# A modulation product whose weight blocks are half split for TensorE, and loaded first

## What is computed

```
shift, scale, gate = silu(c) @ w_ada + b_ada        # w_ada is 1024 x 3072; two conditioning vectors
h = rmsnorm(x) * (1 + scale) + shift
p = h @ w_in                                         # queries, keys, values and gates of two branches
... two attention branches, merge, output projection, residual, final norm
```

## Time and profile before

| | us |
|---|---|
| runs, median (lowest to highest of 3) | 1250.15 (1248.86 to 1251.68) |
| the profiled execution, its own time | 1253.08 |
| its span in the profile | 1251.2 |
| TensorE busy in the span | 1217.1 |
| VectorE busy | 833.5 |
| ScalarE busy | 603.2 |
| mean granted TensorE clock | 0.994 of full |

### The profile page before, as it was taken

One profiled execution on the slowest core, in us unless ns is written; L12 is line 12 of the kernel. 1 busy time (PEld: TensorE's weight loads), 2 busy tenths in 40 slices (PEclk: granted clock), 3 DMA queues, 4 the chain that ended last, 5 costly groups with the idle time before them and its releaser, 6 DMA issues.

```text
span 1251.2 us, 21399 instructions
## 1 busy us (share of the span) xinstructions
PE 1217.1 (97%) x7488; PEld 1087.1 (87%) x7488; DVE 833.5 (67%) x1644; ACT 603.2 (48%) x1207; POOL 189.9 (15%) x203
## 2 busy tenths in 40 slices
PE   7999999999999999999999999999999999999997
PEld 1499889988998999899889989989988898998996
DVE  2368468765875776687687688678768876454452
ACT  3342235544553545265455456546547574443341
POOL 0000023120402130231000000000000025433430
PEclk9999999999999999999999999999999999999999
DMA  9345633132204213221611111321013277543530
GB/s 360 146 175 167 230 109 97 54 132 94 98 34 149 94 69 109 90 96 52 190 62 39 53 39 55 99 69 53 26 51 110 62 242 252 170 147 121 195 141 34
DMA packets 81100, 142.90 MB, mean 114 GB/s; under 512 B 7047, under 2 KB 58119, under 8 KB 81037
## 3 DMA queue, kind: packets, MB, share of 16 engines
q1 hardware_dynamic: 66636, 119.92, 28.7%
q10 hardware_dynamic: 14400, 22.15, 4.9%
HBM read 106.65 MB, written 35.40 MB: 114 GB/s over the span
## 4 chain that ended last, share of the span: by engine, by line
PE 76%; DVE 12%; ACT 4%; issue 4%; DMA 2%; SPq 0%; ACTq 0%; DVEq 0%; POOL 0%
PE d_ps_pairs L86 20%; PE s_ps_pairs L86 11%; PE y_ps L1783 9%; PE b_ps L86 9%; PE o_ps_pairs L1016 7%; PE t_ps_pairs L985 6%; PE v_ps L86 6%; PE s_ps_pairs L944 3%; PE s_ps_pairs L943 3%; DMA wada<-in_w_ada 2%; DVE pt L1335 2%; PE v_ps L299 2%; DVE mn L1345 1%; DVE s_ps_pairs L1352 1%; ACT pr L1141 1%
## 5 line engine op out<-in xcount | busy, mean ns | idle before, releaser
L86 PE MATMUL d_ps_pairs<-h,wt 128*128 128x384 f32 (+2 forms) x1920 | 352.1, 338 | 0.9 <-ACT craw L1159 0.9
L86 PEld LDWEIGHTS d_ps_pairs<-h,wt 128*128 128x128 f32 x1920 | 316.7, 188 | 16.0 <-ACT craw L1159 1.4
L1335 DVE TENSOR_TENSOR pt<-t_ps_pairs,pt 128x512 fp32r<-128x512 f32 (+1 forms) x272 | 157.6, 621 | 39.1 <-ACT pt L1117 37.8
L86 PE MATMUL s_ps_pairs<-h,wt 128*128 128x512 f32 (+1 forms) x864 | 168.4, 354 | 0.0
L1141 ACT ACTIVATE pr<-s_ps_pairs,mx 128x896 f32<-128x896 f32 x128 | 128.2, 1004 | 69.7 <-DVE mx L1361 40.1
L86 PEld LDWEIGHTS s_ps_pairs<-h,wt 128*128 128x128 f32 x864 | 141.6, 189 | 21.7
L1117 ACT ACTIVATE pt<-t_ps_pairs 128x512 fp32r<-128x512 f32 (+1 forms) x272 | 134.1, 548 | 14.8 <-PE t_ps_pairs L985 9.9
L985 PE MATMUL t_ps_pairs<-ident_sb,pr 128*128 128x128 f32 x960 | 131.5, 275 | 3.6 <-DVE pt L1335 2.4
L985 PEld LDWEIGHTS t_ps_pairs<-ident_sb,pr 128*128 128x128 f32 x960 | 107.8, 140 | 14.9 <-DVE pt L1335 10.5
L1783 PE MATMUL y_ps<-wo,mg 128*128 128x512 f32 x480 | 113.2, 396 | 0.0
L1783 PEld LDWEIGHTS y_ps<-wo,mg 128*128 128x128 f32 x480 | 90.0, 188 | 21.6
(11 more groups left out here) (174 smaller groups left out, 1710.3 us busy)
## 6 DMA issues: line engine op xcount, KB each, us to landing
wraw<-in_w_gate SPq DMA_DIRECT2D x24, 512.0 KB, 3.5
gt<-gates_d SPq DMA_DIRECT2D x40, 256.0 KB, 4.3
comb_a<-in_bias SPq DMA_DIRECT2D x24, 384.0 KB, 3.9
gates_d<-craw ACTq DMA_DIRECT2D x48, 192.0 KB, 1.9
vw_a<-v_d SPq DMA_DIRECT2D x64, 128.0 KB
v_d<-vst SPq DMA_DIRECT2D x20, 320.0 KB, 4.6
wada<-in_w_ada SPq DMA_DIRECT2D x12, 512.0 KB, 5.6
oz<-gates_d SPq DMA_DIRECT2D x20, 256.0 KB, 4.4
```

Source lines behind the costliest of these rows:

```text
L86: mm = eng.matmul(out, lhs(a, k), rhs(b, k), start=(k == 0 and i == 0), stop=(k == n_k - 1 and i == 2))
L1335: dve.tensor_tensor(pt[:, 1, c * 512:c * 512 + cols], t_ps[:, n % 2, 0:cols], pt[:, 0, c * 512:c * 512 + cols].bitcast(F32), ALU.subtract) ...
```

## The change

Blocks with an even k in either half (8 of the 16) are no longer multiplied in fp32. ScalarE writes their high part (`mod_high`) and VectorE their low part (`mod_low`), into space of `hm` that is unused at that time. The silu columns are split as well, into a stationary `scl` of 128 by 4 (two high columns, two low columns). A split block is four fp32r products of 512 columns: two chunks, each with the high and the low part of the weight. They write four rows of PSUM; the blocks with an odd k stay in fp32 and add to the first two rows. So four rows are copied to `modrow`, and `columns` turns each 128 of them into two columns by two ordinary fp32 products with parts of the identity, which also add the low rows to the high ones; before it was one transpose.

The loads are put in another order: all 16 modulation blocks, then the key weight, all six value pieces, then the second tokens. The slots are released accordingly: a split block's slot by its low part, an fp32 block's by its products. TensorE now does the columns of the shift half ahead of (1,6), takes (1,5) ahead of (1,4), and does the two first token transposes around the columns of the scale half. ScalarE makes both copies of the shift rows, in place of VectorE; its first squares alternate with `mod_high`. The splits of the first value pieces move: piece 0's and 1's low parts stand between the scale half of `modf` and the first `parts` on VectorE, and piece 2's stands behind the eighth `parts`.

```diff
-    modrow = h32[0:2, :, :]
+    scl = left["scl"]
+    modrow = h32[0:4, :, :]
...
-    SHIFT, KEYS, VALUES0, SCALE, VALUES1 = 0, 8, 9, 12, 20
+    SHIFT, SCALE, KEYS, VALUES = 0, 8, 16, 17
+    MODS = [(0, k) for k in range(KD)] + [(1, k) for k in (0, 1, 2, 3, 5, 4, 6, 7)]
+    SPLIT = [(half, k) for half in range(2) for k in (0, 2, 4, 6)]
...
+    def released(eng, n):
+
+        half, k = n // KD, n % KD
+        if (half, k) in SPLIT:
+            eng.wait_ge(mod_lo, SPLIT.index((half, k)) + 1)
+        elif k == KD - 1:
+            eng.wait_ge(mod_mm, 2 * half + 2)
+        else:
+            eng.wait_ge(ada_used, MODS.index((half, k)) - half + 1)
+
+    def mod_part(j, part):
+
+        return hm[:, part, j, 0:D]
...
         for k in range(4, KD):
             load_ada(0, k)
-        load_keys()
-        for m in range(3):
-            load_v(m)
         for k in range(KD):
             load_ada(1, k)
+        load_keys()
+        for m in range(6):
+            load_v(m)
         load_x(1)
-        for m in range(3, 6):
-            load_v(m)
         sp.wait_ge(wv_lo, 6)
         load_x(2)
...
         def modulation(half, k):
 
-            ring_wait(pe, (SHIFT, SCALE)[half] + k)
+            n = (SHIFT, SCALE)[half] + k
+            if (half, k) in SPLIT:
+                j = SPLIT.index((half, k))
+                pe.wait_ge(mod_lo, j + 1)
+                for c in range(2):
+                    for part in range(2):
+                        mm = pe.matmul(v_ps[0:4, 2 * half + c, :], scl[:, k, :], mod_part(j, part)[:, c * 512:(c + 1) * 512],
+                                       start=(k == 0 and part == 0), stop=False, skip_group_check=True)
+                mm.then_inc(ada_used, 1)
+                return
+            ring_wait(pe, n)
             for c in range(2):
-                mm = pe.matmul(v_ps[0:2, 2 * half + c, :], scol[:, k, :],
-                               ring((SHIFT, SCALE)[half] + k)[:, c * 512:(c + 1) * 512],
-                               start=(k == 0), stop=(k == KD - 1))
-            mm.then_inc(ada_used, 1)
+                mm = pe.matmul(v_ps[0:2, 2 * half + c, :], scol[:, k, :], ring(n)[:, c * 512:(c + 1) * 512],
+                               start=False, stop=(k == KD - 1), skip_group_check=True)
+                if k == KD - 1:
+                    mm.then_inc(mod_mm, 1)
+            if k < KD - 1:
+                mm.then_inc(ada_used, 1)
...
-                mm = pe.transpose(mod_ps[:, 2 * blk:2 * blk + 2], modrow[:, b // 4, (b % 4) * P:(b % 4 + 1) * P],
-                                  ident[0:2, 0:2])
+                for part in range(2):
+                    mm = pe.matmul(mod_ps[:, 2 * blk:2 * blk + 2], modrow[:, b // 4, (b % 4) * P:(b % 4 + 1) * P],
+                                   ident[0:4, 2 * part:2 * part + 2], start=(part == 0), stop=(part == 1))
...
-        pe.wait_ge(silu_done, 1)
-        for k in range(KD):
-            modulation(0, k)
-        pe.wait_ge(ident_in, 16)
-        for k in range(4):
-            modulation(1, k)
-        columns(0)
-        for k in range(4, KD - 1):
-            modulation(1, k)
+        pe.wait_ge(scl_done, 2)
+        for half, k in MODS:
+            if (half, k) == (1, 6):
+                pe.wait_ge(ident_in, 16)
+                columns(0)
+            modulation(half, k)
         transposed(0)
+        columns(1)
         transposed(1)
-        modulation(1, KD - 1)
-        columns(1)
         pe.wait_ge(wk_lo, 1)
...
+        def mod_high(j):
+
+            half, k = SPLIT[j]
+            ring_wait(act, (SHIFT, SCALE)[half] + k)
+            act.activation(mod_part(j, 0), ring((SHIFT, SCALE)[half] + k), ACT.Copy).then_inc(mod_hi, 1)
+
         act.wait_ge(small_in, 32)
         act.activation(scol[:, :, :], ccol[:, :, :], ACT.Silu).then_inc(silu_done, 1)
         act.wait_ge(const_set, 1)
+        mod_high(0)
+        mod_high(1)
         for t in range(XG[0][1]):
             square(0, t)
+            if t < 3:
+                mod_high(t + 2)
+        mod_high(5)
         root(0)
+        mod_high(6)
+        act.wait_ge(mod_mm, 2)
+        for c in range(2):
+            act.activation(modrow[:, c, :], v_ps[0:4, c, :], ACT.Copy).then_inc(mod_row, 1)
+        mod_high(7)
         ring_wait(act, KEYS)
         act.activation(wkb[:, 0, :], ring(KEYS), ACT.Copy).then_inc(wk_hi, 1)
-        for m in range(3):
-            values_high(m)
-        act.wait_ge(ada_used, 2 * KD)
+        values_high(0)
+        act.wait_ge(mod_mm, 3)
         act.wait_ge(mod_col, 1)
-        act.activation(modrow[:, 0, :], v_ps[0:2, 2, :], ACT.Copy).then_inc(mod_row, 1)
+        act.activation(modrow[:, 0, :], v_ps[0:4, 2, :], ACT.Copy).then_inc(mod_row, 1)
+        values_high(1)
         act.wait_ge(mod_ready, 2)
         for i in range(KD):
             modulate(i)
+            if i == 1:
+                values_high(2)
...
+                if g == 0 and t == 2:
+                    mod_low(6)
                 dve.tensor_scalar(x(g)[:, t, :], x(g)[:, t, :], rstd[:, t0 + t:t0 + t + 1], None, ALU.mult
                                   ).then_inc(xn_done, 1)
+
+        def mod_low(j):
+
+            half, k = SPLIT[j]
+            dve.wait_ge(mod_hi, j + 1)
+            dve.tensor_tensor(mod_part(j, 1), ring((SHIFT, SCALE)[half] + k), mod_part(j, 0).bitcast(F32), ALU.subtract
+                              ).then_inc(mod_lo, 1)
 
...
+        dve.wait_ge(silu_done, 1)
+        dve.tensor_copy(scl[:, :, 0:2], scol[:, :, :]).then_inc(scl_done, 1)
+        dve.wait_ge(scl_done, 1)
+        dve.tensor_tensor(scl[:, :, 2:4], scol[:, :, :], scl[:, :, 0:2].bitcast(F32), ALU.subtract).then_inc(scl_done, 1)
+        for j in range(6):
+            mod_low(j)
         normalise(0)
-        dve.wait_ge(small_in, 32)
-        dve.wait_ge(ada_used, KD)
-        for c in range(2):
-            dve.tensor_copy(modrow[:, c, :], v_ps[0:2, c, :]).then_inc(mod_row, 1)
+        mod_low(7)
         dve.wait_ge(wk_hi, 1)
         dve.tensor_tensor(wkb[:, 1, :], ring(KEYS), wkb[:, 0, :].bitcast(F32), ALU.subtract).then_inc(wk_lo, 1)
-        for m in range(3):
-            values_low(m)
+        dve.wait_ge(small_in, 32)
         dve.wait_ge(mod_col, 1)
         dve.tensor_tensor(modf[:, 0:KD, :], mods[:, 0:KD, :], bias[:, 0:KD, :].to_broadcast([P, KD, 2]), ALU.add
                           ).then_inc(mod_ready, 1)
-        dve.wait_ge(ada_used, 2 * KD)
+        dve.wait_ge(mod_mm, 4)
         dve.wait_ge(mod_row, 3)
-        dve.tensor_copy(modrow[:, 1, :], v_ps[0:2, 3, :]).then_inc(mod_row, 1)
+        dve.tensor_copy(modrow[:, 1, :], v_ps[0:4, 3, :]).then_inc(mod_row, 1)
         dve.wait_ge(mod_col, 2)
         dve.scalar_tensor_tensor(out=modf[:, KD:, :], in0=mods[:, KD:, :], scalar=1.0,
                                  in1=bias[:, KD:, :].to_broadcast([P, KD, 2]), op0=ALU.add, op1=ALU.add
                                  ).then_inc(mod_ready, 1)
+        values_low(0)
+        values_low(1)
         for i in range(KD):
             parts(i)
+        values_low(2)
         normalise(1)
...
+            small["scl"] = sb(first, "scl", [P, KD, 4], F32R, "right")
```

More of the change, by code:

```diff
@@ L125, in front @@
     ring_in = [sem(f"ring_in{i}") for i in range(RING)]
-    silu_done, ada_used, mod_row, mod_col, mod_ready = (
-        sem(n) for n in ("silu_done", "ada_used", "mod_row", "mod_col", "mod_ready"))
+    silu_done, scl_done, mod_hi, mod_lo, ada_used, mod_mm, mod_row, mod_col, mod_ready = (
+        sem(n) for n in ("silu_done", "scl_done", "mod_hi", "mod_lo", "ada_used", "mod_mm", "mod_row", "mod_col", "mod_ready"))
     sq_done, rms_done, rstd_done, xn_done, xt_done = (
@@ L150, in ring_wait @@
         eng.wait_ge(ring_in[n % RING], 16 * (n // RING + 1))
+    def released(eng, n):
[8 more added lines that the diff above has]
+        return hm[:, part, j, 0:D]
     def values_raw(n):
         k0, nk = VK[n % 3]
-        return ring(VALUES0 + n if n < 3 else VALUES1 + n - 3)[:, 0:nk * HW].rearrange("p (k c) -> p k c", c=HW)
+        return ring(VALUES + n)[:, 0:nk * HW].rearrange("p (k c) -> p k c", c=HW)
     def values_split(n, part):
@@ L180, in load_ada @@
             n = (SHIFT, SCALE)[half] + k
[L181 to L186, removed]
+            if n >= RING:
+                released(sp, n - RING)
             sp.dma_start(ring(n), io["w_ada"][k * P:(k + 1) * P, half * D:(half + 1) * D]).then_inc(ring_in[n % RING], 16)
         def load_keys():
-            sp.wait_ge(ada_used, KEYS - RING + 1)
+            released(sp, KEYS - RING)
             sp.dma_start(ring(KEYS), io["w_kb"]).then_inc(ring_in[KEYS % RING], 16)
         def load_v(m):
-            n = VALUES0 + m if m < 3 else VALUES1 + m - 3
-            used = n - RING if n < SCALE else KD + n - RING - SCALE
-            sp.wait_ge(ada_used, used + 1)
+            n = VALUES + m
+            released(sp, n - RING)
             k0, nk = VK[m % 3]
@@ L423, in values_high @@
         def values_high(m):
```

(2 more changed lines are left out.)

## The result

| | us |
|---|---|
| before, median of 7 (lowest to highest) | 1250.15 (1248.86 to 1252.51) |
| after, median of 7 (lowest to highest) | 1255.65 (1253.84 to 1257.22) |
| ratio, 95% interval | 1.0043 (1.0031 to 1.0055) |
| profiled execution after: own time, span | 1256.8, 1254.9 |

The kernel became slower by 5.5 us, where I had forecast 1.9 less. The range, 1244.8 to 1252.5, didn't hold it.

What follows compares the result with a forecast made beforehand. TensorE, busy 97% of the span, was taken as the bound. Gain 2.4 up to `modf`, less 1.3 for value splits, plus 0.85 in the loop: 1.95, so 1251.1 us profiled, 1248.2 as median (2.9 lower); range 1244.8 to 1252.5.

Steps and rivals of the forecast that it cites:

- Loads: First stage: in the new load order (1,0) lands at 21.1 instead of 26.0, so the 3.08 us stall goes.
- Splits: Modulation products: a split block costs 0.93 us against 1.72, so eight save 6.3 us of TensorE.
- rival E: Split blocks: a four-column fp32r pass costs an fp32 pass, so six splits save nothing; 1252.9 us, chance 0.03.
- The clock in the stall: Behind the first tokens: TensorE's stall brings one low-clock stretch of 3.4 us, doing 1.7 us less work.
- rival A: Stall at 16 us: TensorE idles under 2 us and the clock survives; gain 3.65, 1246.5 us, chance 0.20.
- The columns' own price: Columns of each half: 32 passes take 3.9 us, standing 0.12 apart.
- Rival B: Columns: passes run at the transposes' pace, 1.6 us less in each half; gain 5.15, 1245.0 us, chance 0.20.
- rival C: Columns: an ordinary fp32 product takes four times a transpose, 4.6 us a half; gain 0.55, 1249.6 us, chance 0.08.
- The value splits: Between `modf` and the first `parts` on VectorE: low parts of pieces 0 and 1 come first, loss 1.3 us.
- The loop: Loop over eight chunks: half of the 1.7 us lost to the low clock comes back, gain 0.85.
- The signs of being wrong: Columns at 0.07 or at least 0.14; from 12 to 40, clock 1.00 or 0.50 for over 6 us; repeated low-part waits.
- Rival D: Clock low from about 18 until 25 behind the stall, and 6.7 us in the loop; 1252.4 us, chance 0.12.

Runs made afterwards that it cites:

- the late columns: The kernel after, with the shift half's columns taken behind (1,7) instead of ahead of (1,6); 1258.04 us, ratio 1.007; its profiled execution took 1253.71.
- the first experiments: Early follow-up measurements, beside which 24 runs of the unchanged kernel before were taken; those runs' mean granted clock was 0.995 to 0.998.

## Why the prediction was wrong, step by step

**Loads: right.** The wait for (1,0) is gone, and no block was late: TensorE's chain from 18.5 to 44 has no DMA in it. The load order alone gave 4.4 us.

**Splits: right in kind, a tenth of a us short per block.** The stall ended at 18.54 (18.3 forecast), ScalarE and VectorE were never late behind it. A split block at full clock took 1.02 to 1.09 (0.93), an fp32 block 1.81 in this stretch (1.72), so rival E is out, and TensorE came to the columns at 34.3 and not at 33.3.

**The clock in the stall: right.** The mean of the first window row is 3.4 low us in five, as assumed; one block took 3.21 instead of 1.81. Six of seven profiled executions with this stall had it; in the seventh (the late columns) it did not come, as rival A had it, though not for A's reason: TensorE idled 2.3 us there too.

**The columns' own price: nearly right.** 32 passes at full clock took 3.67 (the run with the late columns) against my 3.9. Rival B, the transposes' pace (2.3), is out. So is rival C (4.6) at full clock: the traces give a factor of 3, about 0.22 for the two passes of an ordinary product and 0.071 for a transpose. That the kernel after took 4.44 is no point for C, as the clock was halved in the last 1.7 us of it. The rule of the Trainium skill behind it ("TensorE: Matmul & The Clock Gate", Terms) gives a factor of 4. My reason for 0.12, that the weight load sets the pace, isn't shown: a load shows as 187 ns there, and the passes stand 0.112 apart.

**The step that failed** is in the sum behind the columns: "if the clock holds. In the stall it may fall". I let the clock depend on idle stretches of TensorE alone, and counted the time in the columns and behind them as if they were work like any other. They are busy time in every view, and they lowered the clock twice. Measured against forecast, up to `modf`: 1.0 from the blocks before; 0.5 for the first columns (4.44); 2.6 for (1,6) and (1,7), 5.25 instead of 2.65; 0.15 for the token transposes; 0.6 for the second columns (4.49). That is 4.8, and 4.0 of the time spent there is the clock's: 2.4 in the two blocks (5.25 against 1.02 + 1.81) and 0.8 in each half of columns over the 3.67 at full clock.

**The value splits: right.** The first part starts at 51.3, 2.1 us behind the end of `modf`, which is the sum's 0.84 + 1.3 (the "about 3 us" among the signs doesn't fit that sum). Moving them took 1.2 us out of the chain.

**The loop: wrong by sign.** I took 0.85 us back for a low stretch that might not recur. With the second columns in front of it the clock was low from 47.2 on in this profile, for 10 us, and from `modf`'s end to the values it took 14.5 us instead of 12.6; forecast were 13.1.

**From the profile to the median: mis-sized.** I gave the kernel after the 2.9 us by which the profiled execution of before lay above its median; it measured 1.15, which is another 1.8 us. A likely reason, not shown: the chain that I started from held 2.9 us of low clock behind the wait for (1,0), 9.93 for 16 passes that took 7.03 in another execution, and its mean clock of 0.994 lies below all 24 runs of before beside the first experiments. Most executions seem to have had less of that loss, so it could not be won back in full in the median. With this the whole error is accounted for: 4.8 up to `modf`, 1.4 in the loop, 0.6 won back behind it, 1.8 here, together 7.4 of 7.45.

**The signs of being wrong** caught it in part: the clock was low for 6.4 us between 12 and 40 (19.9 to 23.3 and from 37.0 on), where over 6 us was to speak against me.

**Rival D** named the slower side and the low clock in the loop, which it priced 2.55 us above the forecast where 1.4 were measured, but it hung on a long low stretch behind the stall, which did not come, and for the loop on TensorE having nothing to do from 44 to 47, where it was busy without a gap; what lowered the clock was the columns themselves. Its 1252.4 was still 3.3 short. It had 0.12, and the bound that decided it, 10 us of low clock in all, was passed by far (3.4, 6.8 and 10.2 us).

## What to carry to other kernels

Small products that load 128 columns of weights for 2 columns of data are not only dear in themselves: a few us of them lowered TensorE's clock here as idleness does, and the large products behind them paid twice (5.25 us, where they take 2.83 at full clock). Price a rewritten small step by what stands behind it as well, and look at the granted clock over stretches where TensorE shows as fully busy. And when a change has a cheap half (an order of loads) and a dear half (splits by two other engines), measure the cheap half alone: here it gave 4.4 us where the whole cost 5.5. Last, look at the granted clock before carrying one profiled execution's gain over to the median: part of what it shows may be that execution's own.

## What was not expected of the hardware

- The granted clock fell at 37.0 with TensorE busy 2.70 of 2.70 us before it, in matmuls of 2 columns; with four products of 512 columns between every four passes it stayed at 1.00 for 12.4 us, with one it fell. Weight loads alone didn't do it: 22.00 us of them in 22.00, beside products of 256 columns, ran at 1.00.
- An ordinary fp32 product of 4 rows by 128 columns of weights takes two passes of 0.112 at full clock; a transpose of the same block takes 0.072 in all (8 in 0.58).
- After the same idle stretch of about 3 us before (1,0), the clock fell in one execution (8 passes in 6.50) and did not in another (16 in 7.03).
- The column of the granted clock reads 1.00 from 6 to 12 us in the kernel before, though the passes there stand 0.85 apart, twice the 0.43 of full clock. So at the very start of a profile the pace of the passes says more than this column.
